# Reciprocal root of the two feed-forward norms applied to gates and down tiles instead of the input

## What is computed

```
def rms_norm_2(x, g):
    y = xf * lax.rsqrt(jnp.mean(xf * xf, axis=-1, keepdims=True) + RMS_EPS)
    return (y * g.astype(jnp.float32)).astype(x.dtype)

def swiglu(h, w_gate, w_up, w_down):
    return (jax.nn.silu(h @ w_gate) * (h @ w_up)) @ w_down

x = x + 0.5 * swiglu(rms_norm_2(x, ffn1_norm), ...)     # and the same with ffn2
```

## Time and profile before

| what | us |
|---|---|
| median of three runs | 1084.57 (1083.26 to 1085.09) |
| the profiled execution | 1077.73 |
| its span, first to last instruction | 1075.9 |
| PE busy in it | 992.6 |
| POOL busy | 654.8 |
| ACT busy | 535.2 |
| DVE busy | 533.0 |

### The profile page before, as it was taken

One profiled execution on the slowest core, in us unless ns is written; L12 is line 12 of the kernel. 1 busy time (PEld: TensorE's weight loads), 2 busy tenths in 40 slices (PEclk: granted clock), 3 DMA queues, 4 the chain that ended last, 5 costly groups with the idle time before them and its releaser, 6 DMA issues.

```text
span 1075.9 us, 22914 instructions
## 1 busy us (share of the span) xinstructions
PE 992.6 (92%) x9068; PEld 944.6 (88%) x9068; DVE 533.0 (50%) x735; ACT 535.2 (50%) x765; POOL 654.8 (61%) x271
## 2 busy tenths in 40 slices
PE   5998999799799778999999999999999999999996
PEld 5987777698799767899999998999898879999996
DVE  4346424654410895586662003375274668777301
ACT  6565564556554445644444436676331554444441
POOL 2785234356689731698787775554620269888882
PEclk9998999999899899999999999999899999999999
DMA  8553122133355200455555553333300046555551
GB/s 321 195 169 106 60 79 98 59 118 128 127 177 177 79 1 2 149 187 177 177 171 177 176 176 124 117 117 115 99 4 4 23 136 207 188 192 179 192 177 41
DMA packets 38993, 139.79 MB, mean 130 GB/s; under 512 B 4224, under 2 KB 5504, under 8 KB 38784
## 3 DMA queue, kind: packets, MB, share of 16 engines
q1 hardware_dynamic: 38912, 138.62, 38.7%
HBM read 137.55 MB, written 1.05 MB: 129 GB/s over the span
## 4 chain that ended last, share of the span: by engine, by line
PE 55%; issue 21%; POOL 12%; DVE 8%; ACT 2%; DMA 1%; SPq 0%; POOLq 0%; DVEq 0%; ACTq 0%
PE ps L667 55%; POOL wlo L602 11%; DVE qkl L1834 3%; DVE hA L2133 1%; DVE hT L1866 1%; ACT whi L1463 1%; ACT dif L1402 1%; DMA ring<-in_stream 1%; DVE sq L1834 0%; ACT rstd L1402 0%; POOL dif L626 0%; PE ps L1208 0%; DVE hA L1834 0%; DVE rGI L1834 0%; DVE aL L1872 0%
## 5 line engine op out<-in xcount | busy, mean ns | idle before, releaser
L602 POOL TENSOR_TENSOR wlo<-ring,whi 128x1024 fp32r<-128x1024 f32 x251 | 611.8, 2455 | 372.4 <-ACT whi L1463 371.5
L667 PE MATMUL ps<-aH,whi 128*128 128x256 f32 (+1 forms) x1528 | 444.0, 291 | 27.5 <-DVE aL L1834 11.8
L667 PE MATMUL ps<-aH,wlo 128*128 128x256 f32 (+1 forms) x1528 | 438.2, 287 | 0.0
L667 PE MATMUL ps<-aL,whi 128*128 128x256 f32 (+1 forms) x1528 | 437.8, 287 | 0.0
L1463 ACT ACTIVATE whi<-ring 128x1024 fp32r<-128x1024 f32 x253 | 266.3, 1058 | 122.9 <-PE ps L667 107.3
L667 PEld LDWEIGHTS ps<-aH,whi 128*128 128x128 f32 x1528 | 293.4, 192 | 35.3 <-POOL wlo L602 17.6
L667 PEld LDWEIGHTS ps<-aL,whi 128*128 128x128 f32 x1528 | 292.8, 192 | 0.5 <-issue 0.4
L667 PEld LDWEIGHTS ps<-aH,wlo 128*128 128x128 f32 x1528 | 293.1, 192 | 0.0
L667 PE MATMUL ps<-fH,wlo 128*128 128x272 f32 (+1 forms) x352 | 100.8, 286 | 0.0
L667 PE MATMUL ps<-fH,whi 128*128 128x272 f32 (+1 forms) x352 | 100.4, 285 | 0.0
L667 PE MATMUL ps<-fL,whi 128*128 128x272 f32 (+1 forms) x352 | 100.4, 285 | 0.0
(11 more groups left out here) (336 smaller groups left out, 1279.0 us busy)
## 6 DMA issues: line engine op xcount, KB each, us to landing
ring<-in_stream SPq DMA_DIRECT2D x253, 512.0 KB, 3.3
cst<-in_cst SPq DMA_DIRECT2D x1, 1325.0 KB, 13.1
xT<-in_x SPq DMA_DIRECT2D x4, 272.0 KB, 3.7
out<-hT SPq DMA_DIRECT2D x1, 1024.0 KB, 4.6
row<-in_row SPq DMA_DIRECT2D x1, 898.0 KB, 9.7
cst<-in_cst SPq DMA_DIRECT2D x1, 640.0 KB, 10.6
mat<-in_mat SPq DMA_DIRECT2D x1, 576.0 KB, 14.0
vec<-in_vec SPq DMA_DIRECT2D x1, 135.0 KB, 3.8
```

The lines of the kernel that those rows point to most:

```text
L602: nc.gpsimd.tensor_tensor(wlo[:, s, :], ring[:, s, :], whi[:, s, :].bitcast(F32), ALU.subtract).then_inc(S("w_split"), 1)
L667: return nc.tensor.matmul(out, lhsT, rhs, start=start, stop=stop, skip_group_check=True)
```

## The change

For the norms ahead of the two feed-forward parts (`LATE`), rstd is no longer multiplied into the input. ACT writes the high half of `xT * weight` straight from `xT` into a tile of its own (`fxH`), DVE its low half (`fxL`), tile by tile during the projection before. PE takes the first gate-and-up pair, and only then the ones-matmuls, with no filler. The gates are multiplied by rstd in PSUM on DVE ahead of the tanh, for which ACT waits (`ffn_gate`); the up tiles are left as they are, and each output tile of the down projection is multiplied by rstd in PSUM ahead of `xT`. ACT rounds the weights behind the gate unit ahead of that wait, those behind the up unit after the tanh. DVE sums seven tiles of squares in norm0 and ffn1, five elsewhere, and does so behind the `xT` of the tile rather than ahead of it. `fxH` and `fxL` lie where `hT` and `mixT` are.

```diff
+LATE = ("ffn1", "ffn2")
+SUMMED = {"norm0": 7, "norm1": 5, "ffn1": 7, "mix": 5, "ffn2": 5, "final": 5}
...
-            def feature_pair(u, g, t0, ready):
+            def feature_pair(u, g, t0, ready, tag=None):
+                xh, xl = acts(tag)
...
             def norm(tag, n):
                 i = NORMS.index(tag)
                 if i == 0:
                     pe.wait_ge(S("early_in"), 32)
-                else:
+                elif tag not in LATE:
                     filler(1)
-                pe.wait_ge(S("norm_sum"), (SUMMED - 1) * (i + 1))
-                mm(ps[:, 7, 0:n], C("ones"), sq[:, 0, 0:n], True, False)
-                for k in range(SUMMED, KT):
+                pe.wait_ge(S("norm_sum"), sums_up_to(tag))
+                m = mm(ps[:, 7, 0:n], C("ones"), sq[:, 0, 0:n], True, SUMMED[tag] == KT)
+                for k in range(SUMMED[tag], KT):
...
-                if i and tag != "final":
+                if tag in ("norm1", "mix"):
                     filler(3)
...
-                feature_pair(u0, g0, c0, ("norm_h", NORMS.index(tag) * KT))
+                feature_pair(u0, g0, c0, ("norm_h", NORMS.index(tag) * KT), tag)
+                norm(tag, TT - c0)
...
-            norm("ffn1", TT)
             ffn("ffn1", U_F1, G_F1, 0, 0)
...
-            norm("ffn2", T)
             ffn("ffn2", U_F2, G_F2, FT, TM)
...
+                if tag in LATE:
+                    func(acts(tag)[0][:, k, c0:TT], xT[:, k, c0:TT], ACT.Identity, "norm_hi", scale=V(tag, k))
                 func(sq[:, k, 0:n], xT[:, k, c0:c0 + n], ACT.Square, "norm_sq")
...
+                if tag in LATE:
+                    ahead(u0 + n_units - 1)
                 norm(tag, n)
-                ahead(u0 + n_units - 1)
+                if tag not in LATE:
+                    ahead(u0 + n_units - 1)
...
                 def gate(it, f4):
-                    act.wait_ge(S("w_used"), it * 8 + (u0 + 2 * f4 + 1))
+                    ahead(u0 + 2 * f4, it)
+                    act.wait_ge(S("ffn_gate"), it * 4 + (first + f4 + 1))
                     act.wait_ge(S("drained_v"), it * 8 + (d0 + 2 * f4 + 1 - 8))
                     nc.scalar.activation(fth[:, f4, c0:TT], ps[:, (g0 + 2 * f4) % MM_BANKS, 0:TT - c0], ACT.Tanh,
                                          scale=0.5).then_inc(S("ffn_th"), 1)
-                    ahead(u0 + 2 * f4, it)
                     ahead(u0 + 2 * f4 + 1, it)
...
             def residual(tag, g0, c0, scale=1.0):
-                for m in range(KT):
-                    if 2 <= m <= SUMMED:
-                        add_square(tag, m - 1, TT if tag in ("ffn1", "mix") else T)
-                    dve.wait_ge(S("w_used"), used_by(g0 + m))
...
+                wide = TT if tag in ("ffn1", "mix") else T
+                for m in range(KT + 1):
+                    if m < KT:
+                        dve.wait_ge(S("w_used"), used_by(g0 + m))
...
+                        if tag in ("mix", "final"):
+                            tt(out, out, rstd[:, 0:TT - c0], ALU.mult)
+                        stt(xT[:, m, c0:TT], out, scale, xT[:, m, c0:TT], ALU.mult, ALU.add, "drained_v")
+                    if tag in LATE and m >= 1:
+                        low_half(tag, m - 1, wide)
+                    if 2 <= m <= SUMMED[tag]:
+                        add_square(tag, m - 1, wide)
+                if tag in LATE:
+                    dve.wait_ge(S("norm_rstd"), NORMS.index(tag) + 1)
+
+            def low_half(tag, k, n):
+                high, low = [t[:, k, TT - n:TT] for t in acts(tag)]
+                dve.wait_ge(S("norm_hi"), NORMS.index(tag) * KT + k + 1)
+                stt(low, xT[:, k, TT - n:TT], V(tag, k), high.bitcast(F32), ALU.mult, ALU.subtract, "norm_h")
...
                 def pair(it, f4, f):
+                    gate = ps[:, (g0 + 2 * f4) % MM_BANKS, 0:TT - c0]
+                    dve.wait_ge(S("w_used"), it * 8 + (u0 + 2 * f4 + 1))
+                    nc.vector.tensor_tensor(gate, gate, rstd[:, 0:TT - c0], ALU.mult).then_inc(S("ffn_gate"), 1)
                     dve.wait_ge(S("ffn_th"), it * 4 + (first + f4 + 1))
...
-            norm("ffn1", 0, TT, "ffn1")
...
-            norm("ffn2", TM, T, "ffn2")
```

More of the change, by code:

```diff
@@ L91 @@
 MM_BANKS = 4
-SUMMED = 5
 def chunk_bank(c):
@@ L360, with sums_up_to @@
 NORMS = ("norm0", "norm1", "ffn1", "mix", "ffn2", "final")
+LATE = ("ffn1", "ffn2")
+SUMMED = {"norm0": 7, "norm1": 5, "ffn1": 7, "mix": 5, "ffn2": 5, "final": 5}
+def sums_up_to(tag):
+    return sum(SUMMED[n] - 1 for n in NORMS[:NORMS.index(tag) + 1])
 def used_by(g):
@@ L407, in program @@
         xT = sb("xT", [P, KT, TT])
-        hT = sb("hT", [P, KT, TT])
-        mixT = sb("mixT", [P, KT, TT])
+        own = ExitStack()
+        hT = sb("hT", [P, KT, TT], at=own)
+        mixT = sb("mixT", [P, KT, TT], at=own)
+        own.close()
+        fxH = sb("fxH", [P, KT, TT], F32R)
+        fxL = sb("fxL", [P, KT, TT], F32R)
         sq = sb("sq", [P, KT, TT])
@@ L539, in program, with acts @@
         mx.close()
+        def acts(tag):
+            return (fxH[:], fxL[:]) if tag in ("ffn1", "ffn2") else (aH[:], aL[:])
         def V(name, i=0):
@@ L700, in feature_pair @@
                     for wh, wl, b in parts:
-                        m = mm3(ps[:, b, 0:TT - t0], wh[:, k, :], wl[:, k, :], aH[:, k, t0:TT], aL[:, k, t0:TT],
+                        m = mm3(ps[:, b, 0:TT - t0], wh[:, k, :], wl[:, k, :], xh[:, k, t0:TT], xl[:, k, t0:TT],
                                 k == 0, k == KT - 1)
@@ L1045, in gate_up @@
                             at = slice(k * P, (k + 1) * P)
-                            m = mm3(ps[:, (g0 + j) % MM_BANKS, 0:TT - c0], whi[:, s, at], wlo[:, s, at], aH[:, k, c0:TT], aL[:, k, c0:TT],
+                            m = mm3(ps[:, (g0 + j) % MM_BANKS, 0:TT - c0], whi[:, s, at], wlo[:, s, at], xh[:, k, c0:TT], xl[:, k, c0:TT],
                                     k == 0, k == KT - 1)
                         m.then_inc(S("w_used"), 1)
-                feature_pair(u0, g0, c0, ("norm_h", NORMS.index(tag) * KT))
+                feature_pair(u0, g0, c0, ("norm_h", NORMS.index(tag) * KT), tag)
+                norm(tag, TT - c0)
                 for f4 in range(1, 4):
@@ L1415, in norm @@
                 func(rstd[:, 0:n], rstd[:, 0:n], ACT.Exp, "norm_rstd", scale=-0.5)
-                if tag != "final":
+                if tag in ("norm0", "norm1", "mix"):
                     for k in range(KT):
-                        act.wait_ge(S("norm_x"), NORMS.index(tag) * KT + k + 1)
+                        act.wait_ge(S("norm_x"), ("norm0", "norm1", "mix").index(tag) * KT + k + 1)
                         func(aH[:, k, TT - n:TT], hT[:, k, TT - n:TT], ACT.Copy, "norm_hi")
@@ L1853, in norm @@
                 if tag == "norm0":
-                    for k in range(1, SUMMED):
+                    for k in range(1, SUMMED[tag]):
                         add_square(tag, k, n)
@@ L2080, in residual @@
             def residual(tag, g0, c0, scale=1.0):
-                for m in range(KT):
-                    if 2 <= m <= SUMMED:
-                        add_square(tag, m - 1, TT if tag in ("ffn1", "mix") else T)
-                    dve.wait_ge(S("w_used"), used_by(g0 + m))
-                    out = ps[:, (g0 + m // 2) % MM_BANKS, (m % 2) * T:(m % 2 + 1) * T] if tag in ("norm1", "ffn2") else \
-                        ps[:, (g0 + m) % MM_BANKS, 0:TT - c0]
-                    stt(xT[:, m, c0:TT], out, scale, xT[:, m, c0:TT], ALU.mult, ALU.add, "drained_v")
+                wide = TT if tag in ("ffn1", "mix") else T
+                for m in range(KT + 1):
+                    if m < KT:
+                        dve.wait_ge(S("w_used"), used_by(g0 + m))
+                        out = ps[:, (g0 + m // 2) % MM_BANKS, (m % 2) * T:(m % 2 + 1) * T] if tag in ("norm1", "ffn2") else \
+                            ps[:, (g0 + m) % MM_BANKS, 0:TT - c0]
+                        if tag in ("mix", "final"):
[11 more added lines that the diff above has]
+                stt(low, xT[:, k, TT - n:TT], V(tag, k), high.bitcast(F32), ALU.mult, ALU.subtract, "norm_h")
             def hgrn_in():
@@ L2172, in pair @@
                     nc.vector.scalar_tensor_tensor(out=half, in0=fth[:, f4, c0:TT], scalar=1.0,
-                                                   in1=ps[:, (g0 + 2 * f4) % MM_BANKS, 0:TT - c0], op0=ALU.add,
+                                                   in1=gate, op0=ALU.add,
                                                    op1=ALU.mult).then_inc(S("drained_v"), 1)
```

## The result

The changed kernel is slower. Its median is 1127.3 us (1123.9 to 1134.6) against 1084.8 us (1083.3 to 1086.6) for the kernel before on the same chip: ratio 1.040, 95% interval 1.0345 to 1.0455.

The account below looks back on a forecast made before the run. TensorE, busy 92% of the span, was taken as the bound. First block +30.6, second +37.4 and two end multiplies 1.0 us made +69 on 1084.57: 1153.6 us, range 1092 to 1168.

Parts of the forecast that it names:

- The ring: Gate-and-up pairs: VectorE, ScalarE and GpSimd wait for each other in a circle; 7.24 us a turn against TensorE's 6.03 and 5.67.
- One of its signs: Gate-and-up pairs: TensorE would wait about 1.2 to 1.5 us for wlo once in each pair.
- By its first pair: Start of each feed-forward block: the kernel enters the slow 7.24 us turn by its first gate-and-up pair.
- The table loads: Gate phases: every fourth tanh carries a ScalarE table load of 1.28 us, four after the first.
- The last turn: End of each gate phase: counted like every other of 21 turns, at 7.24 us, or 7.2 in the second block.
- The fronts: Norms ahead of ffn1 and ffn2: late weights make TensorE wait; gains only 0.8 and 1.6 us, upper bound 10.95 together.
- The two multiplies at the ends: Last down-projection tile, ahead of mix and of final: multiplying by rstd adds 2 x 0.5 = 1.0 us.
- expected tanh of the last pair: End of the gate phases: tanh of pair 21 at 613.6 in the first block and 1040.0 in the second.
- first tanh: First gate-and-up pair of each block: its tanh at about 456.4 in the first and 883.7 in the second.
- the down phase: Down projection after the last pair's fL: 58.5 us remain in the first block, 54.9 in the second.
- full ring: Gate phases: the slow turn of about 7.2 us holds throughout; 1153.6 us, own range 1140 to 1168, chance 0.66.
- partial ring: Rival, gate phases: the cast wins every second pair, mean turn 6.4 us; 1108 to 1118 us, chance 0.14.

## Why the prediction came out as it did

1. **The ring: right.** The turn was put at 7.24 us and measured 7.21 (7.2 and 7.16 for the narrow tiles). POOL's start 1.42 us behind a tanh and its lead of 0.15 us over the cast were both as read from the earlier trace rows. Shown by four runs: it is there with the multiply alone, gone without the multiply, gone with operands in PSUM, gone with 0.37 us of delay. One of its signs was wrong: PE did wait about once in each pair, but for VectorE to free the gate's bank (half gate, 17.3 us in 18 waits), where I had expected it to wait for wlo.

2. **"By its first pair": half right.** The first block entered at its second pair. The second block ran in the fast pattern first (DVE, kernel after):

```profile
916.18 0.29 DVE L2217 CAST fH<-fact 128x256 f32 x1 [0.17 <-DVE fact L2214]
916.60 2.42 DVE L2219 TENSOR_TENSOR fL<-fact,fH 128x256 f32 x1
...
921.23 0.29 DVE L2217 CAST fH<-fact 128x256 f32 x1 [0.16 <-DVE fact L2214]
...
926.27 2.56 DVE L2217 CAST fH<-fact 128x256 f32 x1 [0.16 <-DVE fact L2214]
```

Behind a first turn of 5.92 us these are turns of 5.06 and 5.04 us, with POOL busy without a gap from 908.87 on and the cast slipping in between two subtractions. I had described this very state (two POOL periods, 4.9 us) as that of the kernel before and had not asked whether the kernel after could be in it. The cast at 926.27 lost its place, and no later one won it back while the loop ran. This took 5.6 us off (three turns of 5.92, 5.06 and 5.04 for 21.6). What made that cast lose is open. The timeline of POOL has subtractions starting at 916.19, 921.24 and 926.28, so all three casts are listed 0.01 us ahead of one; two took 0.29 us and the third 2.56. With the multiply alone the fast pattern was lost one turn later, in the turn after a table load that left POOL idle for 0.27 us: that cast was 0.22 us behind POOL (935.76 against 935.54).

3. **The table loads: mis-sized.** I let four loads of 1.28 us lengthen four turns in each block. Turns with a load were 7.59 to 7.64 us in the first block and 7.43 in the second (7.61 the first of them), 0.4 and 0.27 longer (ACT, kernel after):

```profile
476.69 1.28 ACT L1483 ACT_TABLE_LOAD   x1
477.99 1.06 ACT L1483 ACTIVATE whi<-ring 128x1024 fp32r<-128x1024 f32 x1
482.97 0.40 ACT L1694 ACTIVATE fth<-ps 128x272 f32<-128x272 f32 x1 [3.92 <-DVE ps L2206]
```

The load stands ahead of the first activation of the loop body. With the change that is the gate unit's rounding, done while ScalarE waits 4 to 5 us for the multiply anyway, and no longer the tanh. The remaining 0.4 us comes where VectorE's own loop turns (the multiply at 482.40 had 0.55 us of idle time ahead of it, in place of 0.12); it stayed when ScalarE's loop was written out, and with the load back on the tanh the fourth turn was 7.2 + 1.28 + 0.4 = 8.9. Worth 3.5 us in the first block and 4.0 in the second. The step that failed: I took the place of the load from the kernel before, though the change moves the instruction in front of it.

4. **The last turn: missed.** In both blocks it took 4.76 and 4.65 us, for the last two pairs stand outside the loop (DVE, POOL, kernel after; the tanh was at 599.54):

```profile
599.97 0.44 DVE L2209 SCALAR_TENSOR_TENSOR fhalf<-fth,ps 128x272 f32<-128x272 f32 x1 [0.46 <-ACT fth L1694]
600.44 0.44 DVE L2214 TENSOR_TENSOR fact<-fhalf,ps 128x272 f32<-128x272 f32 x1
600.91 0.30 DVE L2217 CAST fH<-fact 128x272 fp32r<-128x272 f32 x1
...
600.96 2.53 POOL L616 TENSOR_TENSOR wlo<-ring,whi 128x1024 fp32r<-128x1024 f32 x1 [2.42 <-ACT whi L1483]
```

From half gate to cast it is 0.94 us here and 1.14 in the loop: the cast comes at 1.37, 0.05 us ahead of POOL. -2.5 us in each block.

5. **The fronts: small, as put, but by other numbers.** In the first block PE waited 1.8 us and not 3.9. I had let both the low half and the sum of a tile wait for POOL; only the low half did (2.03 us, then the sum 0.43), so VectorE kept PE's pace of 2.9 us for a tile. In the second the wait was 4.13 us against 4.3. But behind both waits PE's clock fell to half. After, granted clock 0.50 in the seventh column:

```profile
443.40:446.40 3.00, 3.00 (x15) 3.00 (x15) 2.93 (x4) 2.02 (x3) 2.59 (x2) 0.50 0.50 176
897.80:900.40 2.60, 2.60 (x15) 2.60 (x14) 2.37 (x4) 0.97 (x3) 1.02 (x1) 0.50 0.57 176
```

That is the lower of its two levels, 1.2 GHz. The wait alone doesn't bring it about: with the product in PSUM the first block has the same wait of 1.78 us, to 448.35, and behind it the full clock:

```profile
448.40:451.40 3.00, 3.00 (x24) 3.00 (x25) 2.93 (x5) 2.09 (x4) 2.50 (x1) 1.00 0.48 172
```

In the kernel after, the lower clock cost this much. The first pair took 450.23 - 442.62 = 7.61 us in place of 6.03, the second block's 903.34 - 896.07 = 7.27 in place of 5.67: 1.6 us lost each. Without the ring the fronts gave 0.6 and -0.4 us, against 0.8 and 1.6 expected. The fillers that the change removes had kept PE at work through most of this time; that the clock held for that reason was not tried.

6. **The two multiplies at the ends: not seen.** The multiply takes 0.45 us and stands ahead of the last xT, so it is inside the blocks and can't be told apart there; what follows the last xT took 0.5 us less than before.

The sum: for each block the expected tanh of the last pair and what follows, against the rows. First block -10.7 us (earlier first tanh -1.6, turns -7.7 of which loads -3.5 and last turn -2.5, the down phase -1.4). Second -12.5 us (turns -12.7, of which the fast start -5.6, loads -4.0, last turn -2.5; front +1.2, down phase -1.0). With +4.0 for the clock in the stage between, which was in no one's forecast, and -1.5 for the ends: +69 becomes +48. The forecast of 1153.6 was 26 us too high, inside the range of 1092 to 1168, but outside the 1140 to 1168 that I gave the full ring: the length of its turn was right to 0.03 us, and how it is entered, the loads and the last turn were not. The range reached below 1140 for the partial ring (1108 to 1118 us), which isn't what ran; that 1127.3 lies in it owes something to luck. The other part of the 26 us is that spans moved by 48.3 us and medians by 42.5.

## What to carry to other kernels

When an edit makes one engine wait for another, draw the whole circle, with the instructions queued behind the wait and the hidden side, an instruction of VectorE and one of GpSimd that can't run together. Then compare the issue times of the two: 0.15 us decided 4% here, and a small delay, or an operand in PSUM, was the cure. And price what stands at the head of a loop body, such as a table load, by the instruction that is first there after the edit.

## What the runs showed of the hardware

- A cast of 272 columns from SBUF to SBUF takes 0.30 us if it is issued 0.05 us ahead of GpSimd's subtraction, and 2.40 us if it is issued 0.15 us behind. Values between come from waiting for the rest of a subtraction already under way. Of three casts of 256 columns listed 0.01 us ahead, two took 0.29 us and one 2.56.
- The same instructions of a loop ran in two patterns (5.05 us for a pair, two or three pairs in a row, and 7.16 us from then on), and within a loop went over only from the fast to the slow one, in the kernel after and with the multiply alone.
- The same VectorE instructions follow each other in 0.94 us outside a hardware loop and in 1.14 inside (half gate to cast), and the turn of VectorE's loop lengthens a pair by 0.3 to 0.4 us.
- 1.78 us without a matmul between a projection and a pair was followed by about 3.4 us at the half clock in the kernel after and by the full clock with the product in PSUM: seven of eight kernels with a wait of 1.76 to 1.84 us there had the half clock behind it.
